# The first feed-forward block of a twelve-stage transformer kernel: modulation and products by slices of 256 channels

## The reference, cut to what matters

```python
c_act = jax.nn.silu(c)                                    # 1024 values
mod = (c_act @ w_ada[l] + b_ada[l]).reshape(B, 9, 1024)
y = x * lax.rsqrt(mean(x * x, axis=-1) + EPS) * norm_gain[l, 0]
h = y * (1 + mod[:, 1]) + mod[:, 0]                       # scale and shift, one value per channel
x = x + 0.5 * mod[:, 2] * ((silu(h @ w_gate) * (h @ w_up)) @ w_down)
```

## Time and profile before

| | us |
|---|---|
| median of 3 runs | 2643.72 (2641.73 to 2644.05) |
| the profiled execution | 2643.91 |
| its span, first to last instruction | 2642.1 |
| PE busy in the span | 2614.3 |
| PE busy in the first 34.03 us | 22.57 |

### The profile page before, as it was taken

One profiled execution on the slowest core, in us unless ns is written; L12 is line 12 of the kernel. 1 busy time (PEld: TensorE's weight loads), 2 busy tenths in 40 slices (PEclk: granted clock), 3 DMA queues, 4 the chain that ended last, 5 costly groups with the idle time before them and its releaser, 6 DMA issues.

```text
span 2642.1 us, 33396 instructions
## 1 busy us (share of the span) xinstructions
PE 2614.3 (99%) x13499; PEld 2184.4 (83%) x13499; DVE 2027.2 (77%) x2314; ACT 1338.6 (51%) x1514; POOL 0.8 (0%) x6
## 2 busy tenths in 40 slices
PE   7999999999999999999999999999999999999998
PEld 4888877888888877888888899888888889997887
DVE  6878888878777888877877767777787786867844
ACT  3445566544445566544544534555454454456543
POOL 0000000000000000000000000000000000000000
PEclk9999999999999999999999999999999999999999
DMA  8986855777776864688687758548768767774752
GB/s 303 321 283 224 285 202 176 257 272 251 269 272 223 297 235 154 231 279 283 222 289 265 262 195 278 186 140 294 266 212 284 266 228 258 237 239 131 249 199 85
DMA packets 316450, 634.17 MB, mean 240 GB/s; under 512 B 12419, under 2 KB 76099, under 8 KB 316297
## 3 DMA queue, kind: packets, MB, share of 16 engines
q1 hardware_dynamic: 303760, 620.78, 68.4%
q10 hardware_dynamic: 12536, 11.25, 1.5%
HBM read 630.88 MB, written 8.97 MB: 242 GB/s over the span
## 4 chain that ended last, share of the span: by engine, by line
PE 94%; DVE 4%; issue 1%; DMA 1%; ACT 0%; SPq 0%; DVEq 0%; ACTq 0%
PE bank L1581 21%; PE bank L1583 20%; PE bank L1582 20%; PE acc L1581 9%; PE acc L1583 9%; PE acc L1582 8%; PE bank L1719 1%; PE bank L1642 1%; DVE w_both L1048 1%; PE bank L1890 1%; DVE softmax L1283 1%; DMA x<-in_x 1%; PE acc L1812 0%; PE bank L1665 0%; PE acc L1872 0%
## 5 line engine op out<-in xcount | busy, mean ns | idle before, releaser
L1048 DVE TENSOR_TENSOR w_both<-raw,w_both 128x2048 fp32r<-128x2048 f32 x412 | 942.0, 2289 | 413.9 <-ACT w_both L607 413.4
L607 ACT ACTIVATE w_both<-raw 128x2048 fp32r<-128x2048 f32 x412 | 786.7, 1913 | 479.4 <-PE bank L1583 314.3
L1581 PE MATMUL bank<-w_both,h 128*128 128x512 f32 x1888 | 750.5, 398 | 2.0 <-DVE h L1154 2.0
L1583 PE MATMUL bank<-w_both,h 128*128 128x512 f32 x1888 | 736.7, 390 | 0.0
L1582 PE MATMUL bank<-w_both,h 128*128 128x512 f32 x1888 | 735.9, 390 | 0.0
L1581 PEld LDWEIGHTS bank<-w_both,h 128*128 128x128 f32 x1888 | 355.0, 188 | 76.5 <-issue 3.7
L1583 PEld LDWEIGHTS bank<-w_both,h 128*128 128x128 f32 x1888 | 354.8, 188 | 75.3
L1582 PEld LDWEIGHTS bank<-w_both,h 128*128 128x128 f32 x1888 | 355.4, 188 | 70.5 <-issue 1.0
L1092 DVE SCALAR_TENSOR_TENSOR ada_sum<-raw,c_act,ada_sum 128x512 f32<-128x512 f32 x476 | 357.5, 751 | 16.5 <-DMA raw<-in_w_ada_all 2.4
L1581 PE MATMUL acc<-w_both,y 128*128 128x512 f32 x896 | 353.3, 394 | 0.0
L1583 PE MATMUL acc<-w_both,y 128*128 128x512 f32 x896 | 349.4, 390 | 0.0
(11 more groups left out here) (219 smaller groups left out, 2393.9 us busy)
## 6 DMA issues: line engine op xcount, KB each, us to landing
raw<-in_w_ada_all SPq DMA_DIRECT2D x136, 1024.0 KB, 5.2
raw<-in_w_in SPq DMA_DIRECT2D x128, 1024.0 KB, 5.4
raw<-in_ffn_down_all SPq DMA_DIRECT2D x88, 1024.0 KB, 5.1
raw<-in_ffn_gate_all SPq DMA_DIRECT2D x80, 1024.0 KB, 5.1
raw<-in_ffn_up_all SPq DMA_DIRECT2D x80, 1024.0 KB, 5.9
raw<-in_ffn_side_all SPq DMA_DIRECT2D x16, 1024.0 KB, 5.2
raw<-in_w_branch SPq DMA_DIRECT2D x12, 1024.0 KB, 7.1
first_w<-in_w_ada_all SPq DMA_DIRECT2D x8, 1024.0 KB, 14.4
```

Source lines behind the costliest of these rows:

```text
L607: activate(halves_of[n][0], src, ACT.Copy).then_inc(high_ready.sem, 1)
L1048: tensor(halves_of[n][1], raw_of("unit", s, k, 0)[0], halves_of[n][0].bitcast(F32), ALU.subtract).then_inc(low_ready.sem, 1)
L1581: mm(dst, a_h, b_h, start=start, stop=False, skip_group_check=True)
L1583: return mm(dst, a_l, b_h, start=False, stop=True, skip_group_check=True)
```

## The change

The first stage takes its channels in four slices of 256. The host lays the columns of `w_ada` out so that group q holds 256 shift and 256 scale columns of slice q (`first_w`, one run of 8 KB per partition and load), and the first four weight units so that unit q holds gate and up weights of slice q (`ffn_first`, 8 KB runs). SP loads x first, then unit q and group q in turn.

x times rstd is turned while the loads run, into `turned_x`. For each group PE takes four tiles of `w_ada` itself (group 0: all eight), with c by a stride of zero as the stationary side, and DVE sums the other four. ACT copies one row of the result (L1006 of the new file), PE turns it to columns by four products of one column (`first_turns`), DVE adds bias and gain in that form, makes h, ACT rounds it, DVE makes its low half. The bias and gain come with the parameter rows; the copy of the gains to 128 partitions, the bias rows and `probs_t` go. PE starts with products of zeros (`keep_busy`), four before and three behind the turn of the parameters. DVE makes the low halves of units 4 and 5 ahead of the first hidden product.

```diff
@@ sync
-            sp.dma_start(tok_f[0:PARAMS, 2048:2048 + P], t["rows"]).then_inc(rows_landed.sem, 16)
+            sp.dma_start(tok_f[0:ROWS, 2048:2048 + P], t["rows"]).then_inc(rows_landed.sem, 16)
...
-            first_load(0)
-            first_load(1)
             sp.dma_start(x[:, :, :], t["x"].rearrange("b (t p) n -> p (b t) n", p=P)).then_inc(x_landed.sem, 16)
-            load(0)
-            load(1)
-            first_load(2)
-            first_load(3)
+            for q in range(4):
+                load(q)
+                first_load(q)
@@ scalar
-            act.dma_start(scale_all[:, :], t["gains"][0, :].partition_broadcast(P)).then_inc(gain_landed.sem, 16)
...
+            def first_highs(q):
+                for tile in (2 * q, 2 * q + 1):
+                    act.wait_ge(first_made.sem, tile + 1)
+                    activate(h_high[:, tile, :], turned_x[:, tile, :], ACT.Copy).then_inc(first_high.sem, 1)
+
+            def first_copy(q):
+                act.wait_ge(first_done.sem, q + 1)
+                activate(first_row(q), first_acc(q)[0:1, :], ACT.Copy).then_inc(first_row_ready.sem, 1)
...
-            shift_out(0)
             high(0, 0)
-            high_of_h(0, 0, 0)
-            high_of_h(0, 1, 0)
-            high(0, 1)
+            first_copy(0)
+            for half in range(2):
+                act.wait_ge(h_turned.sem, h_turned.at(0, h_count(0, 1, half)))
+                activate(turned_x[:, 4 * half:4 * half + 4, tokens(1)], fours(turn_bank(0, 1, half)), ACT.Copy
+                         ).then_inc(x_turned_act.sem, 1)
...
+            first_highs(0)
+            for q in range(1, 4):
+                high(0, q)
+                first_copy(q)
+                first_highs(q)
+            high(0, 4)
+            high(0, 5)
@@ vector
+            def first_slice(q):
+                dve.wait_ge(first_turned.sem, q + 1)
+                linked(tensor(first_mod[:, q], first_columns(q).rearrange("p (a t) -> p a t", a=2),
+                              first_bias[:, :, 2 * q:2 * q + 2], ALU.add))
+                linked(tensor(first_mod[:, q, 1, :], first_mod[:, q, 1, :],
+                              first_params[:, 16 + 2 * q:18 + 2 * q], ALU.mult))
+                if q == 0:
+                    dve.wait_ge(x_turned_dve.sem, 2)
+                    dve.wait_ge(x_turned_act.sem, 2)
+                for i in range(2):
+                    tile = turned_x[:, 2 * q + i, :]
+                    nc.vector.tensor_scalar(tile, tile, first_mod[:, q, 1, i:i + 1], first_mod[:, q, 0, i:i + 1],
+                                            ALU.mult, ALU.add).then_inc(first_made.sem, 1)
+                for tile in (2 * q, 2 * q + 1):
+                    dve.wait_ge(first_high.sem, tile + 1)
+                    tensor(h_low[:, tile, :], turned_x[:, tile, :], h_high[:, tile, :].bitcast(F32), ALU.subtract
+                           ).then_inc(first_h.sem, 1)
...
+            low(0, 0)
+            first_slice(0)
+            for q in range(1, 4):
+                first_sum(q, range(4))
+                low(0, q)
+                first_slice(q)
+            low(0, 4, with_sums=False)
+            low(0, 5)
@@ tensor
+                    last = mm(first_acc(q), c_act[:, 0, k:k + 1].to_broadcast([P, P]), first_w[:, q, k, :],
+                              start=k == (0 if q == 0 else 4), stop=False, skip_group_check=True)
...
+            def first_turns(q):
+
+                pe.wait_ge(first_row_ready.sem, q + 1)
+                for j in range(4):
+                    last = mm(first_columns(q)[:, j:j + 1], first_row(q)[:, P * j:P * j + P], ones[0:1, 0:1],
+                              start=j == 0, stop=j == 3, skip_group_check=True)
+                last.then_inc(first_turned.sem, 1)
...
                 def first_block():
...
+                    for q in range(3):
+                        first_group(q, 0, 0)
+                        first_direct(q + 1, range(4, 8))
+                        first_summed(q + 1, 4 * (q + 1))
+                        first_group(q, 0, 1)
+                        first_turns(q + 1)
+                        first_group(q, 1, 0)
+                        first_group(q, 1, 1)
+                    first_group(3, 0, 0)
+                    first_group(3, 0, 1)
+                    first_group(3, 1, 0)
                     turn_hidden(0, 0)
-                    up(0, 1, 1)
+                    first_group(3, 1, 1)
...
+            def keep_busy(count):
+                for _ in range(count):
+                    mm(bank[0][:, :], seed[:, 0:P], seed[:, :], start=True, stop=True)
```

More of the change, by code:

```diff
@@ L438, in unit_source @@
         def unit_source(s, k):
-            if s == 0:
-                k = {1: 2, 2: 1}.get(k, k)
+            if s == 0 and k < 4:
+                return t["ffn_first"][k], 2
             layer, l = s // 3, (s // 3) % 2
@@ L1210, in ffn @@
                 product(0, 0)
-                low(s, 4)
                 if s == 0:
+                    sums(s, 4)
                     product(0, 1)
                     low_of_hidden(0, 0)
-                    low(s, 5)
                     low(s, 6)
@@ L1220, in ffn @@
                 else:
+                    low(s, 4)
                     low(s, 5)
@@ L1541, in _ @@
[L1541 to L1551 removed]
+            dve.wait_ge(params_ready.sem, 1)
+            linked(nc.vector.tensor_scalar(first_params[:, 8:16], first_params[:, 8:16], 1.0, None, ALU.add))
@@ L1557, in _ @@
                    ).then_inc(table_ready.sem, 1)
-            low_of_h(0, 1, 0)
-            low(0, 1)
-            first_sum(2, range(4, 8))
-            first_sum(3, range(8))
-            first_scale(1)
-            normed_half(0, 0, 1)
-            low(0, 2)
-            low_of_h(0, 0, 1)
-            normed_half(0, 1, 1)
-            low(0, 3)
-            low_of_h(0, 1, 1)
+            dve.wait_ge(zeros_ready.sem, 2)
+            for tt in range(TT):
+                spread(0, tt)
+                for half in range(2):
+                    nc.vector.tensor_scalar(half_of(work, tt, half), half_of(x, tt, half), rstd[:, tt:tt + 1], None,
+                                            ALU.mult).then_inc(normed.sem, 1)
+            for half in range(2):
+                dve.wait_ge(h_turned.sem, h_turned.at(0, h_count(0, 0, half)))
+                nc.vector.tensor_copy(turned_x[:, 4 * half:4 * half + 4, tokens(0)], fours(turn_bank(0, 0, half))
+                                      ).then_inc(x_turned_dve.sem, 1)
+            low(0, 0)
[6 more added lines that the diff above has]
+            low(0, 5)
             for s, kind in enumerate(STAGES):
@@ L1727, in down, with first_group @@
                              last=n == LAST and part == PARTS[n] - 1, halves=halves)
[L1729 to L1744 removed]
+                def first_group(q, tt, is_up):
+                    wh, wl = weights(s, q, 2)
+                    c = slice(512 * is_up, 512 * is_up + 512)
+                    for i in range(2):
+                        tile = 2 * q + i
+                        pe.wait_ge(first_h.sem, tile + 1)
+                        last = triple(bank[2 * is_up + tt][:, :], h_high[:, tile, tokens(tt)], h_low[:, tile, tokens(tt)],
+                                      wh[:, i, c], wl[:, i, c], tile == 0)
+                    if tt and is_up:
+                        last.then_inc(used.sem, 1)
+                    elif q == 3 and not tt:
+                        last.then_inc(part_done.sem, 1)
+                def first_block():
+                    pe.wait_ge(table_ready.sem, 2)
+                    for q in range(3):
[9 more added lines that the diff above has]
+                    first_group(3, 1, 0)
                     turn_hidden(0, 0)
[L1746 removed]
+                    first_group(3, 1, 1)
                 def other_block():
@@ L2146, in _ @@
                ).then_inc(params_turned.sem, 1)
-            pe.wait_ge(c_spread.sem, 1)
-            pe.wait_ge(bias_row_landed.sem, 32)
-            def first_seeds(q):
-                mm(first_acc(q), ones[0:1, :], first_bias[q], start=True, stop=False, skip_group_check=True)
-            first_seeds(0)
-            first_seeds(1)
-            first_direct(1, range(4))
-            first_summed(0, 8)
-            first_summed(1, 12)
-            first_seeds(2)
-            first_seeds(3)
-            turn_h(0, 0, 0)
+            pe.wait_ge(c_ready.sem, 1)
+            first_direct(0, range(4))
+            for half in range(2):
+                turn_h(0, 0, half)
+            first_direct(0, range(4, 8)).then_inc(first_done.sem, 1)
+            for half in range(2):
+                turn_h(0, 1, half)
+            first_turns(0)
+            for half in range(2):
+                pe.wait_ge(x_turned_act.sem, half + 1)
+                pe.wait_ge(x_turned_dve.sem, half + 1)
             for s, kind in enumerate(STAGES):
@@ L2216 @@
         "rel_rows": np.ascontiguousarray(a["rel_bias"].reshape(16, REL)[:, ::-1]),
```

(6 more changed lines are left out.)

111 lines of the change are left out of this document (41 added, 70 removed).

## The result

| us | before | after |
|---|---|---|
| median | 2641.77 (2641.43 to 2644.05, 12 runs) | 2648.85 (2647.14 to 2650.37, 12 runs) |
| profiled execution, span | 2643.91, 2642.1 | 2649.05, 2647.3 |
| first product with h | 34.03 | 26.06 |
| unit 4 | 63.24 | 68.48 |

The account below looks back on a forecast made before the run. PE, busy 2614.3 of 2642.1 us, bounds the kernel, so only unit 4's start matters. It moves -0.5 at full clock, plus 2.3 and 0 to 1.6 for clock falls: middle +2.6, 2646.5 us; range 2641.0 to 2650.5.

Parts of the forecast that it names:

- the mark: Start of unit 4, the first product behind the rewritten block: 63.24 us before, forecast at 64 to 67.
- the sum with its clock cases: Start of unit 4: -0.5 us at full clock, +2.3 for the first gap, 0 to 1.6 for another: +1.8 to +3.4.
- the rival for that side: DVE late for a slice, a low half standing before it: up to 2.3 us per slice, 2649.7 us; chance 0.13.
- three slow gaps: Clock falls at PE's gaps before 13.4, from 21.1 to 24.3, and before the hidden turn; 60%, 50%, 35% likely.
- The slow stretch: Start: the gap from about 10.2 to 13.4 us slows four fp32 products, costing 2.3 us; 60% likely.
- The stretch from there to the mark: First product with h to unit 4: 21.9 + 12.8 + 1.5 + 0.4 + 1.8 = 38.4 us, ending at 62.7.
- the sets of turns: One-column turns of slices 1 to 3, eight instructions each: 0.5 us a set, 1.5 together, bounds 0.6 to 2.7.
- The hidden wait: End of the block: PE waits 1.8 us for DVE's hidden product, made behind both low halves.
- The case that the range's lower end of 2641.0 was said to take in: Zeros hold the clock, turns cost 0.2 us a set and PE has no wait at the end.
- the first gap: PE idle from the table product, about 10.2 us, to 13.4, 3.2 us; a clock fall there 60% likely, costing 2.3.
- That zeros don't raise the clock: Start: products of zeros leave the clock low, first fp32 product at 14.9 and slow; +3.3 to +4.9, 2648 us; chance 0.13.
- That they hold it over the gap: Start: zeros keep the clock up until 13.4 us, so the gap costs nothing; 2643.4 to 2645.0 us; chance 0.17.

Follow-up runs that it names:

- a4_no_direct: Changed kernel without the twelve fp32 products of groups 1 to 3 that PE makes between the products with h; 2641.19 us, 0.9997 of before.
- a1_fill_gap: Changed kernel with two more products of zeros in front of the first fp32 products of group 0; 2645.96 us, 1.0015 of before.
- a6_two_ahead: Changed kernel with two of group 1's four fp32 products moved ahead of the first product with h; 2645.55 us, 1.0008 of before.
- a7_five_tiles: Changed kernel with DVE summing five tiles of groups 1 to 3 instead of four, PE making three fp32 products; 2644.95 us, 1.0008 of before.
- a5_turn_mode: Changed kernel with the four turns of a slice's row in transpose mode, one instruction each instead of two; 2646.49 us, 1.0011 of before.
- a3_hidden_first: Changed kernel with token tile 0's hidden product before unit 5's low half, and ACT's silu before unit 5's rounding; 2647.18 us, 1.0017 of before.
- b1_before_filled: Kernel before the change with four fp32 products of a constant put in PE's two gaps, into unused banks; 2641.81 us, 0.9998 of before.

## Why the prediction was right, and where its sizes were short

**Direction and mechanism held.** The start became 8 us shorter (26.06 against 34.03), and the fp32 products, now among the products with h, paid it back: they measure 10.3 us there, and a4_no_direct, which leaves them out, is 6.3 us shorter to the mark, with 2.3 of waiting for DVE and a longer slow stretch in their place. The time, 2648.85, lies in the range of 2641.0 to 2650.5, but 2.35 above the forecast, and the mark moved by 5.24 where the sum with its clock cases gave 1.8 to 3.4. The ratio of 1.0022 stands at the border of the slower side of 0.2%, which I gave 0.17. It did not get there by the rival for that side: DVE was late for no slice, as the waits show. That the time lies inside the range is in part luck, since the upper end was made of three slow gaps with turns at 0.9, and what came was two slow gaps with turns at 1.26.

**The first product with h** was put at 24.3 and came at 26.06. The load landed at 12.64, not 13.4 (-0.8). The slow stretch, a case of its own in the forecast, took 1.8. The chain from the one-column turns to the first product took 26.06 - 23.12 = 2.94, not 2.3 (+0.6). The turns end 1.1 behind their start, as ACT's copies did in the sum. The two small adds on DVE take 0.4 (24.20 to 24.60), which the sum had between slices and left out here, and from the scale and shift on it is 1.46 instead of 1.2: 256 columns are 0.37, not 0.27.

**The stretch from there to the mark** was put at 38.4 at the full clock and took 42.42. The term that was mis-sized is the sets of turns: 0.5 each in the sum, 0.2 to 0.9 in the bounds, 1.26 measured, three times +0.76 = +2.3. Both bounds came from rows of wide products, and neither held it. A slow stretch is +1.7. The hidden wait was 1.54 for 1.8, -0.3. Some 0.3 is left unassigned. The case that the range's lower end of 2641.0 was said to take in gives 2640.7 by its own terms (-0.5 - 0.9 - 1.8 against 2643.9). Without the two slow stretches the mark would have moved by 5.24 - 1.8 - 1.7 = +1.7 instead of the -0.5 of the sum; a1_fill_gap, with no fall, has it at +1.9.

**The clock.** The forecast had the first gap slow and one of the others "possibly". The profiled execution had the first and the second, each at 1.7 to 1.8 (I had 2.3 and 1.6, the first from 4.6 us at 1.2 GHz, where 3.4 were measured); the third, the hidden wait, brought no fall in any profiled execution. Of the twelve products behind 49.71 that I call slow in before, the first three ran ahead of the fall; the 1.6 lost over the twelve stands. The first product with h came where the text said to look (24 to 27); the mark, at 68.48, missed its 64 to 67 by 1.5.

**The rivals.** That zeros don't raise the clock is refuted by the table product, 0.82 us with them and 1.47 without. That they hold it over the gap is true in part of the executions: the profiled ones of a6_two_ahead and a7_five_tiles show it, and after's lower cluster, about 2 us below the other, would be such executions, by its times.

**The two pages.** The eight instructions of a set, 1.05 us busy, are 0.13 us each, so the floor of about 25 ns that the Trainium skill states (TensorE: Matmul & The Clock Gate, section Wait — 56ns, not 53.3ns?) is not what binds here, and the sum by that floor would have been further off. The loads, most of them now with 8 KB per partition, ran at 419 GB/s over the stretch of 4 to 36 us of after:

```profile
4.00:36.00 32.00, 28.36 (x86) 14.77 (x84) 14.29 (x31) 12.86 (x26) 0.00 (x0) 0.89 1.02 419
```

The HBM limit of about 358 GB/s for a core in the Trainium skill (DMA: Bandwidth & Descriptors, section Specifications) is passed again; the measurement decides.

## What to carry to other kernels

Before work is moved out of an engine's idle time to shorten the path to a first result, ask what that work costs where it now stands: here 8 us at the start were bought with 10 us of fp32 products and 4 us of turns in a stretch where PE has next to no idle time. When a restructured start leaves PE a gap, put into it first the real work of the next step (two products of group 1 took 1.7 us off the path), and only then a filler. Price tiny instructions by a row of tiny instructions, or leave a bound wide enough for a fixed cost per instruction.

## What the runs showed of the hardware that was not expected

- A one-column fp32 product is two instructions of about 0.13 us each: 1.05 us for the eight of a set in after. In transpose mode it is one, and the four of a set take 0.40 us (a5_turn_mode).
- The clock at a gap was not set by the length of that gap alone, though the longest two are the ones that held. After PE's idle time in front of the first fp32 product it fell in after (1.74 us), a3_hidden_first (1.4), a4_no_direct (1.7) and a5_turn_mode (1.8), and not in the profiled executions of a6_two_ahead (2.50 us) and a7_five_tiles (2.2). At the second gap it held over 1.90 us of idle in a1_fill_gap, and fell over the same 1.90 in after. The two that held had risen earlier: from the same start at 1.34 us, their first four products of zeros took 5.20 and 5.37 us, where the four that fell took 6.11 to 6.32 (and a1_fill_gap, which held with the gap filled, 6.21). So kernels with the same list up to there differ from execution to execution. What decides it stays open.
- When the clock fell, it stayed down for 3.4 us both times in after, and for 6.8 us in a4_no_direct (27.0 to 33.8) behind the same gap, with a wait for DVE inside. In before it was down for 6.8 us too (26.6 to 33.4), and for 3.4 in b1_before_filled (26.3 to 29.7).
- DVE's scale and shift of 256 columns costs 0.37 us (0.74 for two), where the one-scalar form over 512 takes 0.49; if the two forms cost alike per column, some 0.25 of either is a fixed part, an estimate from these two alone.
